# Stick-breaking attention: the running sums as two single-pass products of a split softplus

## What is computed

```
def stick_breaking_attention(q, k, v):
    """q, k, v: (B, S, H, D). A[t,s] = beta_ts * prod_{s<j<t}(1 - beta_tj), s < t."""
    ...
        z = jnp.einsum('bqhd,bkhd->bhqk', qb, k).astype(jnp.float32) * scale
        mask = (k_pos[None, :] < q_pos[:, None])[None, None]
        log_1mb = jnp.where(mask, jax.nn.log_sigmoid(-z), 0.0)
        rem = lax.cumsum(log_1mb, axis=3, reverse=True) - log_1mb
        a = jnp.where(mask, jnp.exp(jax.nn.log_sigmoid(z) + rem), 0.0)
        return jnp.einsum('bhqk,bkhd->bqhd', a.astype(v.dtype), v)
```

## Time and profile before

| | before |
|---|---|
| three timed executions, median | 2151.29 us |
| the profiled execution, its own time | 2154.26 us |
| its span in the trace | 2152.2 us |
| stick heads, first product to the last running sum's end | 1640.8 to 1716.5 us |
| TensorE busy | 2079.8 us, 97% |
| mean granted TensorE clock | 0.987 of full |

### The profile page before, as it was taken

One profiled execution on the slowest core, in us unless ns is written; L12 is line 12 of the kernel. 1 busy time (PEld: TensorE's weight loads), 2 busy tenths in 40 slices (PEclk: granted clock), 3 DMA queues, 4 the chain that ended last, 5 costly groups with the idle time before them and its releaser, 6 DMA issues.

```text
span 2152.2 us, 42058 instructions
## 1 busy us (share of the span) xinstructions
PE 2079.8 (97%) x17490; PEld 1248.7 (58%) x17490; DVE 863.2 (40%) x1471; ACT 456.9 (21%) x740; POOL 359.6 (17%) x389
## 2 busy tenths in 40 slices
PE   6999999999999999999999999979999999999998
PEld 5888767343443443344343333337776777888887
DVE  4454434523333332332332332333565443544444
ACT  4252433000000000000000000023444522212211
POOL 1010000122223222232222222231201200000000
PEclk9999999999999999999999999979999999999999
DMA  6334112999999999999999999973111021232231
GB/s 236 107 118 146 59 40 99 417 402 403 405 411 404 404 410 405 402 409 403 398 407 403 403 409 394 400 249 108 59 60 40 1 79 59 95 100 97 82 111 41
DMA packets 157313, 520.50 MB, mean 242 GB/s; under 512 B 16412, under 2 KB 71760, under 8 KB 124400
## 3 DMA queue, kind: packets, MB, share of 16 engines
q1 hardware_dynamic: 136480, 494.96, 58.7%
q0 software_dynamic: 20784, 24.85, 4.8%
HBM read 509.61 MB, written 18.88 MB: 246 GB/s over the span
## 4 chain that ended last, share of the span: by engine, by line
PE 79%; DMA 9%; SPq 4%; DVE 3%; ACT 2%; issue 1%; POOL 1%; ACTq 0%; DVEq 0%; POOLq 0%
PE ps L2026 23%; PE ps L392 12%; PE ps L394 12%; PE ps L393 12%; PE ps L2040 11%; DMA ring_a<-in_w_gate_up 5%; DMA ring_a<-in_w_down 4%; SPq L567 2%; SPq L569 2%; PE ps L1902 1%; PE ps L494 1%; PE ps L1955 1%; PE ps L1912 1%; POOL rstd L466 1%; PE ps L1754 1%
## 5 line engine op out<-in xcount | busy, mean ns | idle before, releaser
L2026 PE MATMUL ps<-ring_a,xe 128*32 128x512 f32 x3912 | 432.9, 592 | 2.2 <-DMA ring_a<-in_w_gate_up 2.2
L2040 PE MATMUL ps<-ring_a,act_t 128*32 128x256 f32 x6000 | 333.5, 379 | 5.6 <-DMA ring_a<-in_w_down 3.8
L2026 PEld LDWEIGHTS ps<-ring_a,xe 128*32 128x32 f32 x3912 | 124.5, 110 | 284.1 <-issue 250.6
L2040 PEld LDWEIGHTS ps<-ring_a,act_t 128*32 128x32 f32 x6000 | 192.8, 110 | 153.9 <-issue 21.4
L2026 PE MATMUL ps<-ring_b,xe 128*32 128x512 f32 x2232 | 251.5, 593 | 0.0
L392 PE MATMUL ps<-xt_hi,hi 128*128 128x512 f32 x576 | 227.3, 395 | 1.5 <-DVE ff_a L1655 0.8
L394 PE MATMUL ps<-xt_hi,lo 128*128 128x512 f32 x576 | 225.2, 391 | 0.0
L393 PE MATMUL ps<-xt_lo,hi 128*128 128x512 f32 x576 | 225.1, 391 | 0.0
L1089 ACT ACTIVATE glu<-glu 128x768 f32<-128x768 f32 x32 | 27.0, 843 | 648.0 <-DVE glu L1609 648.0
L759 POOL DMA_INDIRECT x_rows<-ye,idx x96 | 154.3, 1608 | 37.9 <-issue 37.9
L2026 PEld LDWEIGHTS ps<-ring_b,xe 128*32 128x32 f32 x2232 | 68.9, 110 | 149.5 <-issue 142.2
(11 more groups left out here) (298 smaller groups left out, 2464.6 us busy)
## 6 DMA issues: line engine op xcount, KB each, us to landing
ring_a<-in_w_gate_up SPq DMA_DIRECT2D x163, 1024.0 KB, 22.2
ring_a<-in_w_down SPq DMA_DIRECT2D x125, 1024.0 KB, 24.4
ring_b<-in_w_gate_up SPq DMA_DIRECT2D x93, 1024.0 KB, 20.2
raw<-in_w_in SPq DMA_DIRECT2D x20, 1024.0 KB, 7.6
raw<-in_w_gate SPq DMA_DIRECT2D x11, 1024.0 KB, 5.3
raw<-in_w_up SPq DMA_DIRECT2D x11, 1024.0 KB, 5.3
raw<-in_w_down SPq DMA_DIRECT2D x11, 1024.0 KB, 4.9
raw<-in_w_out SPq DMA_DIRECT2D x8, 1024.0 KB, 5.1
```

The source lines that it names most:

```text
L2026: last = pe.matmul(ps[QUAD * j:QUAD * j + QUAD, g, :], xe[:, g, QUAD * k:QUAD * k + QUAD], w[:, j, :, :, :], start=k == 0, stop=k == KT - 1)
L2040: last = pe.matmul(y_block(g, j), act_t[:, g, QUAD * (2 * c + h):QUAD * (2 * c + h) + QUAD], w[:, h, QF * j:QF * j + QF], start=c == 0 and ...
```

## The change

The running sums take the softplus in two parts. ScalarE copies the masked `sp` to `sp_hi`, rounded to fp32r (`stick_hi`), and VectorE writes the difference to `sp_lo` (`stick_lo`); `sp_hi` lies where `z_e` lay and `sp_lo` where `sp` lay. The triangle and the ones are copied once to fp32r (`tri`). TensorE then runs twenty fp32r products per head in place of ten float32 ones, and waits for `sp_lo` of the head. The softplus now waits for each tile's logarithm and no longer for all four. GpSimd masks the softplus of head h+1 ahead of the weights of head h, and `keep_warm` behind the logits of head 1 has six products in place of four. Two semaphores of other stages are merged into others, with the same order.

```diff
@@ gpsimd
             for h in range(SH):
+                if h + 1 < SH:
+                    mask_softplus(h + 1)
                 pool.wait_ge(s_a, T * (h + 1))
...
-                if h + 1 < SH:
-                    mask_softplus(h + 1)
@@ scalar
-                    i = act.activation(z_e[:, h % 2, j, 0:w], z_e[:, h % 2, j, 0:w], ACT.Ln, bias=1.0)
-                i.then_inc(s_ln, 1)
+                    act.activation(z_e[:, h % 2, j, 0:w], z_e[:, h % 2, j, 0:w], ACT.Ln, bias=1.0).then_inc(s_ln, 1)
+
+            def stick_hi(h):
+                act.wait_ge(s_spm, h + 1)
+                for j in range(T):
+                    w = SEQ - P * j
+                    copy(sp_hi[:, h % 2, j, 0:w], sp[:, h % 2, j, 0:w]).then_inc(s_hi, 1)
...
+            copy(tri[:, :], const[:, C_NTRI:C_NTRI + 2 * P])
             stick_exp(0)
             stick_ln(0)
...
+            stick_hi(0)
             for h in range(SH):
...
                 stick_a(h)
+                if h + 1 < SH:
+                    stick_hi(h + 1)
@@ vector
             def stick_softplus(h):
-                dve.wait_ge(s_ln, h + 1)
...
+                    dve.wait_ge(s_ln, T * h + j + 1)
...
+            def stick_lo(h):
+                for j in range(T):
+                    w = SEQ - P * j
+                    dve.wait_ge(s_hi, T * h + j + 1)
+                    i = dve.tensor_tensor(sp_lo[:, h % 2, j, 0:w], sp[:, h % 2, j, 0:w], sp_hi[:, h % 2, j, 0:w].bitcast(F32),
+                                          ALU.subtract)
+                i.then_inc(s_lo, 1)
...
                 if h >= 4:
                     stick_scale(h - 4)
+                if h < SH:
+                    stick_lo(h)
@@ tensor
-                pe.wait_ge(s_spm, h + 1)
+                pe.wait_ge(s_lo, h + 1)
                 for j in range(T):
                     for m in range(j, T):
-                        last = mm(stick_z(h, j)[:, (m - j) * P:], cc(C_NTRI if m == j else C_NONES),
-                                  sp[:, h % 2, m, 0:SEQ - m * P], start=False, stop=True, skip_group_check=True)
+                        for part_ in (sp_hi, sp_lo):
+                            last = mm(stick_z(h, j)[:, (m - j) * P:], tri[:, 0:P] if m == j else tri[:, P:2 * P],
+                                      part_[:, h % 2, m, 0:SEQ - m * P], start=False, stop=True, skip_group_check=True)
...
-                    keep_warm(pe, 7, 4)
+                    keep_warm(pe, 7, 6)
```

More of the change, by code:

```diff
@@ L242, in program @@
         sp = at("sp", HT + 16 * KB, [P, 2, T, SEQ])
+        sp_hi = at("sp_hi", HT, [P, 2, T, SEQ], F32R)
+        sp_lo = at("sp_lo", HT + 16 * KB, [P, 2, T, SEQ], F32R)
+        tri = at("tri", 120 * KB, [P, 2 * P], F32R)
         a_sb = at("a_sb", K(40), [P, 2, T, SEQ])
@@ L333, in program @@
         x_set = sem("x_rows_set")
[L334 to L339, removed]
+        bd_done, comb, f_ss, f_rstd, f_x = (sem(f"final_{s}") for s in
+            ("bias", "sum", "squares", "rstd", "x"))
+        rel_dma, rel_flip, rel_f, rel_fs, lam_s, lam_e = (sem(f"rel_{s}") for s in
+            ("dma", "turned", "f", "f_sb", "lambda_sums", "lambda_exp"))
         hn_sq, hn_ss, hn_var, hn_rstd = (sem(f"head_norm_{s}") for s in ("squares", "sums", "variance", "rstd"))
@@ L347, in program @@
              "out", "out_evacuated"))
+        s_hi, s_lo = (sem(f"stick_{s}") for s in ("softplus_hi", "softplus_lo"))
         f_raw = [sem(f"f_raw_loaded{i}") for i in range(RAW)]
@@ L689, in final_rstd @@
                 pool.tensor_scalar(var[:, 50 + t:51 + t], ss[:, 50 + t:51 + t], 1.0 / D, EPS_1,
-                                   ALU.mult, ALU.add).then_inc(f_var, 1)
-                pool.wait_ge(f_var, t + 1)
+                                   ALU.mult, ALU.add).then_inc(mix_mean, 1)
+                pool.wait_ge(mix_mean, t + 2)
                 inverse_root(pool, rstd[:, 50 + t:51 + t], var[:, 50 + t:51 + t]).then_inc(f_rstd, 1)
@@ L1293, in vector_program @@
             link(dve.tensor_tensor(tiny[:, 44:45], tiny[:, 43:44], tiny[:, 42:43], ALU.subtract))
-            dve.tensor_scalar(tiny[:, 45:46], tiny[:, 44:45], LAMBDA_INIT, None, ALU.subtract).then_inc(lam_r, 1)
+            link(dve.tensor_scalar(tiny[:, 45:46], tiny[:, 44:45], LAMBDA_INIT, None, ALU.subtract))
             def combine(t):
@@ L1369, in scale_heads @@
                                   ALU.mult).then_inc(y_n, 1)
-            dve.wait_ge(lam_r, 1)
             diff_logits(0)
```

## The result

The changed kernel took 2158.20 us, median of seven executions (2155.66 to 2160.00), against 2151.65 for the kernel before in the same rounds: ratio 1.0029, 95% interval 1.0019 to 1.0038. It is slower by 0.29%. The profiled execution is the slowest of the seven. The prediction was 2150.5 with a range to 2154.2: wrong, 4 us past the upper end.

What follows compares the result with a forecast made beforehand. TensorE bound the stage at 9.06 us a head, then a cross-engine loop at 7.5. Terms -3.6 (order and products), +1.6 (blocking) and +1.2 (clock) gave -0.8: 2150.5 us, range 2147.0 to 2154.2.

Steps and rivals of the forecast that it cites:

- +1.2: TensorE gap ahead of head 1's sums: clock falls and slows part of the following work, 1.2 us, bounds 1.0 to 2.5.
- The second fall: Rival, chance 0.12: TensorE's idle ahead of head 7's sums brings 1.2 GHz; those sums lose 1.4, total +0.6, 2151.9 us.
- the clock stays low: Slower rival: TensorE stays at 1.2 GHz behind the first gap; two heads give +6.5, 2157.8; chance 0.07 including old-price products.
- The two added `keep_warm` products end before head 0's sums can start: nothing.: Opening, TensorE: added products end at 1650.7 against 1651.6, cost nothing; without that cover 1.7 us.
- The twenty products: TensorE's running sums: twenty fp32r products take 2.74 us a head in place of 4.53; bounds 2.34 and 4.53.
- Narrow products are quick: Rival, chance 0.10: width-128 products cost 0.06, TensorE takes 6.9 a head, saved in opening and last head; -4.5, 2146.8 us.
- 7.27: TensorE's predicted work per head in us: sums 2.74, values 2.18, logits 2.35; not the bound.
- The loop: VectorE, ScalarE, GpSimd from softplus through mask and copy to subtractions: sets the head period at 7.5 us, before 9.06.
- +1.6: Heads 4 to 7: GpSimd's mask and VectorE's scale block each other, about 0.4 us four times; bounds 0 and 2.4.
- The opening: Heads 0 to 2: scaling block delays head 1's `stick_lo`; head 2's sums start 5.2 us late.
- The norm's factor blocks: Rival, chance 0.04: GpSimd's norm factor holds VectorE off during subtractions; five heads lose 0.8 each, +3.2, 2154.5 us.

Runs made afterwards that it cites:

- fill_last: Changed kernel plus three `keep_warm` products ahead of head 7's running sums only; 2152.99 us, ratio 0.9999 to the kernel before.
- spread_mid: Changed kernel, scaling block spread over heads 1 to 3, older heads' sums and scale moved before the softplus, five `keep_warm` products added; 2146.53 us, ratio 0.9970.
- spread_mid_bare: `spread_mid` without its five added `keep_warm` products; 2154.34 us, ratio 1.0010 to the kernel before.
- fill_both: Changed kernel plus six `keep_warm` products ahead of head 1's sums and three ahead of head 7's; 2152.41 us, ratio 0.9999.
- mask_late: `fill_both` with GpSimd's softplus mask back behind the weights' mask, as before the change; 2160.66 us, ratio 1.0042.
- old_products: `fill_first` with ten float32 products per head on `sp_lo` alone in place of twenty split ones, results wrong; 2163.51 us, ratio 1.0053.
- spread_fill: Changed kernel, scaling block spread over heads 1 to 3, `keep_warm` added: one behind head 1's logits, one ahead of head 1's sums, three ahead of head 7's; 2149.29 us.
- half_products: `fill_both` with only the high part's ten products in the running sums; 2159.58 us, ratio 1.0038.
- fill_first: Changed kernel plus six `keep_warm` products ahead of head 1's running sums only; 2153.06 us, ratio 1.0009.

## Why the prediction was wrong

- **The step that failed is the clock, in two places.** The sum had "+1.2" for one fall, in the gap ahead of head 1's sums; head 1's sums alone lost 2.4, since they ran at half clock almost throughout. The second fall was a rival with a chance of 0.12, priced at +1.4 for head 7's sums. It came, and cost 2.5 there, 3.9 in the values and 0.6 in the last `keep_warm`. 9.4 of clock against 1.2 is nearly the whole error of the stage, which is 7.6 longer where 0.8 shorter was predicted; `fill_last` gave 6.8 us of the stage back with three products, and `spread_mid` against `spread_mid_bare` 7.3 with five. The price of 1.4 was wrong before any run: work of 2.74 us takes 5.48 at half clock, so it costs 2.7 more and not half of 2.74. The rival "the clock stays low" has the same slip in its two heads.
- **Why the price was low.** I took the length of a low stretch from one row (6.7 us) and thought that steady work would end it. Ahead of head 7's sums lie 2.64 us of nothing, and behind its sums only narrow values, which kept TensorE busy for 8.5 us without ending the low clock. How long a low stretch lasts is not fixed: 3.4 to 17.1 us behind nearly the same gap. The profiled execution had the longest of them, so its 9.4 are not the price in every execution. The Trainium skill (TensorE: Matmul & The Clock Gate, Why this matters for your kernels) asks for no idle gaps over about 3 us between bursts. The second gap is shorter and the clock fell anyway, and in `fill_both` it fell after 2.6 us of unbroken work, the nearest gap being 1.13 us long; here the rows decide.
- **"The two added `keep_warm` products end before head 0's sums can start: nothing."** Right for the chain, but they left a gap of 1.39 us, and the fall near 1657.4 stayed when the later gap was filled. That this gap is its cause is not shown, and alone it is not enough: `mask_late` and `old_products` had it and no fall near there, `spread_fill` had it down to 0.53, put another product ahead of head 1's sums, and had one. `spread_mid` left it, put a product on each side of head 2's logits, and had no fall.
- **The twenty products.** 2.74 predicted, 2.82 measured from start to start and 2.92 in the chain: the first product of a head is 0.11 dearer, two others about 0.05, and most of the narrow pairs are 0.05 cheaper. "Narrow products are quick" was wrong in sum. Right was that TensorE would not be the bound at 7.27; with 7.50 both bounds coincide, which `spread_mid` reached.
- **The loop.** 7.5 predicted without blocking and 7.9 with it; measured 7.86, four times between the subtractions of head 3 and those of head 7. The scale took 0.74 for 0.42, 0.3 each, as the +1.6 had it.
- **The opening.** `sp_lo` of head 1 from 1660.83, and head 2's sums 7.8 us later from the stage's start than before (27.5; now 35.3), of which 2.4 are clock: 5.4 against the predicted 5.2.
- **"The norm's factor blocks" and "the clock stays low".** The subtractions took 1.68 beside a GpSimd power of 1.33, and 1.69 at 1660.83 with none: they were not blocked. The slower rival named the right engine and a price of the right order (2157.8), but placed it behind the first gap, where the clock came back.

The -1.8 without the clock is also near what the filled kernels give: `fill_last` has a stage of +0.7 against before with 2.4 us of clock in head 1's sums, so -1.7; `fill_both` has -0.4 with head 1's sums 0.9 late, so -1.3. A few tenths are not accounted for. What stays open is what exactly ahead of 1657 makes the clock fall, and what sets the length of a low stretch; no run changed the opening alone, and each kernel has one trace.

## What to carry to other kernels

When an engine that was never idle gets less to do, look at what it does in the waits that appear: here -1.8 us of order and products became +7.6 through TensorE's clock, and what helped was five products that nobody reads, together with a shorter loop. Price a low clock on all that TensorE does for as long as a low stretch may last (here 3.4 to 17.1 us, once 30.7), and not on the one instruction behind the gap. And before an instruction is put into a loop that runs over several engines, look for the wait in that loop in which the older heads' work can stand; that was worth 0.36 us a head.

## What the hardware showed unexpectedly

- Busy is not enough to raise the clock. TensorE was busy without a break for 8.5 us with products of width 64, and for 30.5 us in `half_products` with a mix of widths, and stayed at 1.2 GHz; it was back about 2 us after `keep_warm` products of width 512 began (the changed kernel: from 1727.1, back at 1729.1; `half_products`: from 1714.6, back at 1716.6).
- Half the products in the sums made the kernel slower: 2159.58 against 2152.41 us.
- The same TensorE instructions behind the same gap of 2.6 us had a low stretch of 17.1 us in one traced execution and of 3.4 in another (the changed kernel and `fill_first`).
- A split product of width 128 follows the one before it after 0.06 or 0.11 us by turns, though each loads 128 columns of weights.
- A mask on GpSimd and a scale on VectorE, overlapping, both grew (0.64 to 0.82, 0.42 to 0.74); a GpSimd power of 128x4 beside the subtractions left them at 1.68, and itself took 1.33 there against 1.01 to 1.19 behind head 7's sums. The Trainium skill (SBUF — State Buffer, Who interferes with whom) has the first one hold the shared pair for the whole instruction; the masks agree with a lock of that kind, the subtractions beside the power do not.
